# A gated-convolution and attention trunk on one core: the opening of the first layer rebuilt in column quarters

## The reference

```python
mod = silu(c) @ ada_w[l] + ada_b[l]
sh_m, sc_m, g_m, sh_f, sc_f, g_f = split(mod, 6)
h = rms_norm(x, norm_mix_g[l]) * (1 + sc_m) + sh_m
# layer 0: u = h @ sc_w_in[0]; [b_g, c_g, xv] = split(u, 3)
#          y = (b_g * causal_conv3(c_g * xv)) @ sc_w_out[0]
x = x + g_m * y
h = rms_norm(x, norm_mlp_g[l]) * (1 + sc_f) + sh_f
x = x + g_f * (relu(h @ mlp_w1[l]) ** 2 @ mlp_w2[l])
```

## Time and profile before

| | us |
|---|---|
| median of 3 runs (1244.55 to 1245.02) | 1244.95 |
| the profiled execution | 1245.44 |
| its span | 1243.6 |
| PE busy, share of the span | 1188.2, 96% |
| DVE busy, share | 775.5, 62% |
| ACT busy, share | 489.5, 39% |

### The profile page before, as it was taken

One profiled execution on the slowest core, in us unless ns is written; L12 is line 12 of the kernel. 1 busy time (PEld: TensorE's weight loads), 2 busy tenths in 40 slices (PEclk: granted clock), 3 DMA queues, 4 the chain that ended last, 5 costly groups with the idle time before them and its releaser, 6 DMA issues.

```text
span 1243.6 us, 16742 instructions
## 1 busy us (share of the span) xinstructions
PE 1188.2 (96%) x5738; PEld 985.6 (79%) x5738; DVE 775.5 (62%) x1101; ACT 489.5 (39%) x797; POOL 24.7 (2%) x37
## 2 busy tenths in 40 slices
PE   4399999999999999999989999999999999999998
PEld 3288888878888888888868888888888888888887
DVE  5655698886576665555878888787843443443441
ACT  4132242443232232332467777774542232332331
POOL 2000000000000000002020000000000000000000
PEclk9699999999999999999999999999999999999999
DMA  9445666455665656333244455450233333333332
GB/s 338 137 156 200 203 191 192 143 153 190 181 214 176 189 199 202 97 90 87 60 111 120 118 125 131 120 153 18 77 97 98 102 94 92 101 101 86 100 101 85
DMA packets 227294, 168.71 MB, mean 136 GB/s; under 512 B 5316, under 2 KB 206188, under 8 KB 227244
## 3 DMA queue, kind: packets, MB, share of 16 engines
q1 hardware_dynamic: 226684, 165.88, 44.8%
q10 hardware_dynamic: 528, 2.10, 0.5%
q0 software_dynamic: 32, 0.07, 0.0%
HBM read 153.24 MB, written 2.10 MB: 125 GB/s over the span
## 4 chain that ended last, share of the span: by engine, by line
PE 80%; DVE 10%; ACT 4%; issue 3%; DMA 2%; SPq 1%; DVEq 0%; ACTq 0%
PE bank L540 24%; PE bank L542 24%; PE bank L541 24%; PE bank L807 2%; DVE ada_acc L1445 1%; PE bank L789 1%; PE bank L753 1%; DMA raw<-in_sc_w_in 1%; DVE w_lo L1313 1%; DVE h_lo L1362 1%; ACT w_hi L947 1%; DVE ta L1353 1%; PE bank L779 1%; DVE tc L1353 1%; PE bank L780 1%
## 5 line engine op out<-in xcount | busy, mean ns | idle before, releaser
L540 PE MATMUL bank<-h_hi,w_hi 128*128 128x512 f32 (+1 forms) x872 | 340.1, 390 | 23.1 <-DVE h_lo L1362 20.1
L541 PE MATMUL bank<-h_lo,w_hi 128*128 128x512 f32 (+1 forms) x872 | 332.6, 381 | 0.0
L542 PE MATMUL bank<-h_hi,w_lo 128*128 128x512 f32 (+1 forms) x872 | 332.6, 381 | 0.0
L947 ACT ACTIVATE w_hi<-raw 128x1024 fp32r<-128x1024 f32 x188 | 197.4, 1054 | 262.8 <-DMA raw<-in_mlp_w 218.3
L540 PE MATMUL bank<-g_hi,w_hi 128*128 128x512 f32 (+1 forms) x688 | 263.3, 383 | 2.3 <-DVE g_lo L1362 1.5
L1313 DVE TENSOR_TENSOR w_lo<-raw,w_hi 128x1024 fp32r<-128x1024 f32 x188 | 229.4, 1223 | 52.4 <-ACT w_hi L947 47.3
L542 PE MATMUL bank<-g_hi,w_lo 128*128 128x512 f32 (+1 forms) x688 | 257.8, 375 | 0.0
L541 PE MATMUL bank<-g_lo,w_hi 128*128 128x512 f32 (+1 forms) x688 | 257.6, 374 | 0.0
L540 PEld LDWEIGHTS bank<-h_hi,w_hi 128*128 128x128 f32 x872 | 164.9, 189 | 61.1 <-issue 22.9
L541 PEld LDWEIGHTS bank<-h_lo,w_hi 128*128 128x128 f32 x872 | 165.2, 189 | 31.9 <-issue 1.9
L542 PEld LDWEIGHTS bank<-h_hi,w_lo 128*128 128x128 f32 x872 | 164.9, 189 | 31.6
(11 more groups left out here) (172 smaller groups left out, 996.0 us busy)
## 6 DMA issues: line engine op xcount, KB each, us to landing
raw<-in_mlp_w SPq DMA_DIRECT2D x128, 512.0 KB, 4.0
ada_raw<-in_ada_w SPq DMA_DIRECT2D x40, 1024.0 KB, 6.0
raw<-in_sc_w_in SPq DMA_DIRECT2D x24, 512.0 KB, 4.0
ada_first<-in_ada_w SPq DMA_DIRECT2D x16, 512.0 KB, 8.9
raw<-in_w_kv SPq DMA_DIRECT2D x16, 512.0 KB, 4.1
raw<-in_sc_w_out SPq DMA_DIRECT2D x8, 512.0 KB, 4.0
raw<-in_q_w SPq DMA_DIRECT2D x8, 512.0 KB, 4.8
keys<-qk SPq DMA_DIRECT2D x16, 256.0 KB
```

Source lines behind the costliest of these rows:

```text
L540: mm(out[:, cols], weights_hi, hi[:, k, cols], start=(k == 0), stop=False)
L541: mm(out[:, cols], weights_hi, lo[:, k, cols], start=False, stop=False)
L542: return mm(out[:, cols], weights_lo, hi[:, k, cols], start=False, stop=(k == KT - 1))
L947: go(w_hi[:, jj, :, :], raw[:, jj, :, :], ACT.Copy).then_inc(hi_ok, 1)
```

## The change

The first stage is done in four quarters of 256 columns. x comes over SP's queue in four row pieces, ahead of all else; the rows for c, the first norm and the modulation's bias come over ACT's queue; the other rows are loaded and transposed later. ACT squares x by token rows with a running sum, the root is taken on 128 by 4 values, and the token rows are scaled (two by DVE, two by ACT) into x_unit, which PE transposes; ACT turns the transposed tile into h with one scale and shift from PSUM, and copies h_hi. x itself is still transposed and copied, with its own banks. The modulation comes in 32 pieces of 256 KB; DVE takes five pieces of quarter 0 and seven of each other, PE multiplies the remaining ones by silu(c) directly, four products of one column for each piece, and adds DVE's sum with products by ones into the same four columns. Blocks 0 to 3 are open at the same time in banks 0 to 3. Block 4 has buffers of its own (early_raw, early_hi, early_lo) and is split before block 0 is finished. The c_g steps are written out; from step 2 on DVE splits before it does its modulation step. mlp_gain and its like are called after the add of step 3, ahead of that step's weight split.

The diff, cut to its core (its lines moved to the left):

```diff
+QUARTERS = 4
+X_BANK = [0, 1, 2, 3, 7, 7, 7, 7]
+ADA_STEPS = [(0, 1, 2, 3, 4)] + 3 * [tuple(range(KT - 1))]
+ADA_DIRECT = [tuple(k for k in range(KT) if k not in steps) for steps in ADA_STEPS]
+STEP_NO = {(q, k): n for n, (q, k) in enumerate((q, k) for q in range(QUARTERS) for k in ADA_STEPS[q])}
+DIRECT_NO = {(q, k): n for n, (q, k) in enumerate((q, k) for q in range(QUARTERS) for k in ADA_DIRECT[q])}
...
-ada_first, = stacked(region_g, [("ada_first", [P, KT, 2, D // 2], F32)])
+ada_first, = stacked(region_g, [("ada_first", [P, 2, KT, 2, D // QUARTERS], F32)])
...
+c_g = columns(sc_w_in[0], D)
+for t in range(TT):
+    sp.dma_start(x_rows[:, t, :], x_in[0, t * P:(t + 1) * P, :]).then_inc(x_loaded[t], 16)
+def ada_quarter(q):
+    for k in range(KT):
+        if (q - 2, k) in STEP_NO:
+            sp.wait_ge(ada_stepped, STEP_NO[q - 2, k] + 1)
+        elif q >= 2:
+            sp.wait_ge(ada_direct, DIRECT_NO[q - 2, k] + 1)
+        src = ada_w[0, k * P:(k + 1) * P, 0:2 * D].rearrange("p (a q c) -> p a q c", a=2, q=QUARTERS)
+        sp.dma_start(ada_first[:, q % 2, k, :, :], src[:, :, q, :]).then_inc(ada_in[q % 2][k], 16)
+for q in range(QUARTERS):
+    ada_quarter(q)
+    if q < 2:
+        load_block(2 * q, c_g(2 * q))
+        load_block(2 * q + 1, c_g(2 * q + 1))
+sp.wait_ge(hi_ok, 1)
+sp.dma_start(early_raw[:], c_g(GROUP)).then_inc(raw_in[0], 16)
...
-for s in range(2):
-    ada_pair(s, 0, 2, s)
-for s in range(GROUP):
+sp.wait_ge(unit_turned, KT)
+ada_pair(0, 0, 2, 0)
+for s in range(1, GROUP):
     sp.wait_ge(pe_done, s + 1)
     load_block(s, c_g(GROUP + s))
-    if s % 2:
-        sp.wait_ge(ada_used, 2 * KT + s + 1)
-        ada_pair(s // 2, 0, 2, 2 + s // 2)
+    if s == 2:
+        ada_pair(1, 0, 2, 1)
+for s in range(2):
+    sp.wait_ge(ada_used, 2 * KT + 2 * s + 2)
+    ada_pair(s, 0, 2, 2 + s)
 blocks(KT, KT, columns(sc_w_in[0], 2 * D), (0, 3))
...
-pe.wait_ge(rows_in, 16 * 11)
-turn(bank[7][:, 0:ROWS], rows_a[:], ident[0:ROWS, 0:ROWS]).then_inc(cols_pe, 1)
+pe.wait_ge(rows_in, 16 * 3)
+turn(bank[7][:, 0:R_MLP], rows_a[0:R_MLP, :], ident[0:R_MLP, 0:R_MLP]).then_inc(cols_pe, 1)
...
+def unit_pair(q):
+    for i in range(2):
+        j = 2 * q + i
+        if q:
+            pe.wait_ge(hs_ok, j - 1)
+        for t in range(TT):
+            if j == 0:
+                pe.wait_ge(*((unit_ok, t + 1) if t < 2 else (unit_rest_ok, t - 1)))
+            v = turn(bank[4 + i][:, t * P:(t + 1) * P], x_unit[:, t, j * P:(j + 1) * P], ident[:])
+        v.then_inc(unit_turned, 1)
+def quarter_direct(q):
+    if q:
+        pe.wait_ge(ada_red, q)
+    for k in ADA_DIRECT[q]:
+        pe.wait_ge(ada_in[q % 2][k], 16 * (q // 2 + 1))
+        for n in range(4):
+            one = mm(bank[6][:, n:n + 1], ada_first[:, q % 2, k, n // 2, n % 2 * P:(n % 2 + 1) * P],
+                     c_act[:, k:k + 1], start=(k == ADA_DIRECT[q][0] and n == 0), stop=False,
+                     skip_group_check=True)
+        one.then_inc(ada_direct, 1)
+def quarter_sum(q):
+    pe.wait_ge(ada_stepped, STEP_NO[q, ADA_STEPS[q][-1]] + 1)
+    for n in range(4):
+        c = n // 2 * KT + 2 * q + n % 2
+        one = mm(bank[6][:, n:n + 1], ada_acc[:, c * P:(c + 1) * P], ones[:, 0:1], start=False,
+                 stop=True, skip_group_check=True)
+    one.then_inc(ada_turned, 1)
+def x_turn(j):
+    if j == 4:
+        pe.wait_ge(cols_ok, 1)
+    if j > 4:
+        pe.wait_ge(x_ok, j)
     for t in range(TT):
+        if j == 0:
+            pe.wait_ge(x_loaded[t], 16)
+        v = turn(bank[X_BANK[j]][:, t * P:(t + 1) * P], x_rows[:, t, j * P:(j + 1) * P], ident[:])
     v.then_inc(x_turned, 1)
-        add_square(j - 2)
-add_square(KT - 2)
-add_square(KT - 1)
+def open_block(b, tiles):
+    last = part_of(b, b, bank[b], h_hi, h_lo, tiles, lambda k: pe.wait_ge(h_ok, H_MIX0 + k + 1))
+    if tiles[-1] == KT - 1:
+        last.then_inc(pe_done, 1)
 pe.wait_ge(cols_ok, 2)
-ada_turn(0, ADA_HALF)
+pe.wait_ge(c_ok, 1)
+Q = [range(2 * q, 2 * q + 2) for q in range(QUARTERS)]
+for j in range(5):
+    x_turn(j)
+quarter_direct(0)
+unit_pair(0)
+quarter_sum(0)
+x_turn(5)
+pe.wait_ge(x_ok, 4)
+open_block(0, Q[0])
+unit_pair(1)
+quarter_direct(1)
+quarter_sum(1)
+open_block(1, Q[0])
+x_turn(6)
+open_block(0, Q[1])
+open_block(1, Q[1])
+unit_pair(2)
+quarter_direct(2)
+quarter_sum(2)
+open_block(2, Q[0])
+open_block(2, Q[1])
+open_block(3, Q[0])
+x_turn(7)
+open_block(3, Q[1])
+open_block(0, Q[2])
+open_block(1, Q[2])
+unit_pair(3)
+quarter_direct(3)
+quarter_sum(3)
+open_block(2, Q[2])
+open_block(3, Q[2])
+for tile in Q[3]:
+    for b in range(2):
+        open_block(b, range(tile, tile + 1))
+open_block(2, Q[3])
+open_block(3, Q[3])
+pe.wait_ge(rows_more, 16 * 8)
 pe.wait_ge(x_ok, KT)
-ada_turn(ADA_HALF, ADA_GATE)
+turn(bank[7][:, 0:ROWS], rows_a[:], ident[0:ROWS, 0:ROWS]).then_inc(cols_pe, 1)
+dense(1, 0, h_hi, h_lo, weights=(early_hi[:].rearrange("p (s k) c -> p s k c", s=1),
+                                 early_lo[:].rearrange("p (s k) c -> p s k c", s=1)))
+for jj in range(1, GROUP):
+    dense(1, jj, h_hi, h_lo)
...
+def token_square(t):
+    act.wait_ge(x_loaded[t], 16)
+    go(x_unit[:, t, :], x_rows[:, t, :], ACT.Square, accum_out=tok[:, 0, t:t + 1]).then_inc(ms_ok, 1)
+token_square(0)
 act.wait_ge(cols_ok, 1)
 go(c_tmp[:], cols[:, R_C:R_C + KT], ACT.Exp, scale=-1.0).then_inc(silu_e, 1)
+for t in range(1, TT):
+    token_square(t)
+act.wait_ge(consts, C_EPS)
+act.wait_ge(ms_ok, TT)
+link(go(tok[:, 1, :], tok[:, 0, :], ACT.Ln, bias=eps_col[:], scale=1.0 / D))
+go(tok[:, 1, :], tok[:, 1, :], ACT.Exp, scale=-0.5).then_inc(norm_y, 1)
+act.wait_ge(inv_ok, 1)
+for t in range(2, TT):
+    go(x_unit[:, t, :], x_rows[:, t, :], ACT.Copy, scale=tok[:, 3, t:t + 1]).then_inc(unit_rest_ok, 1)
+def first_tile(j):
+    act.wait_ge(unit_turned, j + 1)
+    act.wait_ge(mod_ok, j // 2 + 1)
+    if j >= 4:
+        act.wait_ge(h_ok, H_MIX0 + j - 3)
+    go(hs_slot(j, ALL), bank[4 + j % 2][:], ACT.Identity, bias=mcol(0, 0, j),
+       scale=gains[:, 0, j:j + 1]).then_inc(hs_ok, 1)
+    act.wait_ge(hs_ok, H_MIX0 + j + 1)
+    go(h_hi[:, j, :], hs_slot(j, ALL), ACT.Copy).then_inc(hh_ok, 1)
+def x_tile(j):
     act.wait_ge(x_turned, j + 1)
+    go(x[:, j, :], bank[X_BANK[j]][:], ACT.Copy).then_inc(x_ok, 1)
+def split_early():
+    act.wait_ge(raw_in[0], 32)
+    go(early_hi[:], early_raw[:], ACT.Copy).then_inc(hi_ok, 1)
+split(0, 0)
+for j in range(5):
+    x_tile(j)
+first_tile(0)
+first_tile(1)
+split(0, 1)
+x_tile(5)
+first_tile(2)
+first_tile(3)
+split(0, 2)
+x_tile(6)
+split(0, 3)
+first_tile(4)
+first_tile(5)
+x_tile(7)
+split_early()
+first_tile(6)
+first_tile(7)
...
 def step_cg(g, jj, j):
     act.wait_ge(pe_done, 4 * g + jj + 1)
     go(z[:, bass.ds(j, 1), CONV - 1:] if not isinstance(j, int) else z[:, j:j + 1, CONV - 1:],
        bank[jj][:].rearrange("p (a t) -> p a t", a=1), ACT.Copy).then_inc(bank_free, 1)
-    split(g, jj + 3)
+    if j >= 2:
+        split(g, jj + 3)
...
+def quarter_steps(q, first, last):
+    acc = ada_acc[:, 0:2 * D].rearrange("p (a q c) -> p a q c", a=2, q=QUARTERS)[:, :, q, :]
+    for k in ADA_STEPS[q][first:last]:
+        dve.wait_ge(ada_in[q % 2][k], 16 * (q // 2 + 1))
+        row = ada_first[:, q % 2, k, :, :]
+        if k == 0:
+            one = ts(acc, row, c_act[:, 0:1], None, ALU.mult)
+        else:
+            dve.wait_ge(ada_stepped, STEP_NO[q, k])
+            one = stt(out=acc, in0=row, scalar=c_act[:, k:k + 1], in1=acc, op0=ALU.mult, op1=ALU.add)
+        one.then_inc(ada_stepped, 1)
+def quarter_gain(q):
+    both = lambda t: t[:, 0:2 * KT].rearrange("p (a b) -> p a b", a=2)[:, :, 2 * q:2 * q + 2]
+    dve.wait_ge(ada_turned, q + 1)
+    tt(both(mod), bank[6][:, 0:4].rearrange("p (a b) -> p a b", a=2), both(ada_bias),
+       ALU.add).then_inc(ada_red, 1)
+    dve.wait_ge(ada_red, q + 1)
+    gain(0, 0, 1, R_MIX, q + 1, (2 * q, 2 * q + 2))
+def first_low(j):
+    h_low(H_MIX0 + j, j, None, h_hi, h_lo)
+def split_early():
+    dve.wait_ge(hi_ok, GROUP + 1)
+    tt(early_lo[:], early_raw[:], early_hi[:], ALU.subtract).then_inc(lo_ok, 1)
...
+quarter_steps(0, 0, 2)
+dve.wait_ge(norm_y, 1)
+total, y, half_y2, inv = (tok[:, n, :] for n in range(4))
+link(stt(out=half_y2, in0=y, scalar=-0.5, in1=y, op0=ALU.mult, op1=ALU.mult))
+ts(total, total, 1.0 / D, EPS, ALU.mult, ALU.add).then_inc(norm_v, 1)
+dve.wait_ge(norm_v, 1)
+link(tt(half_y2, half_y2, total, ALU.mult))
+stt(out=inv, in0=half_y2, scalar=1.5, in1=y, op0=ALU.add, op1=ALU.mult).then_inc(inv_ok, 1)
+dve.wait_ge(inv_ok, 1)
+dve.wait_ge(ms_ok, TT)
+for t in range(2):
+    ts(x_unit[:, t, :], x_rows[:, t, :], tok[:, 3, t:t + 1], None, ALU.mult).then_inc(unit_ok, 1)
+quarter_steps(0, 2, 5)
+split(0, 0)
+quarter_gain(0)
+quarter_steps(1, 0, 2)
+first_low(0)
+quarter_steps(1, 2, 3)
+first_low(1)
+split(0, 1)
+quarter_steps(1, 3, KT)
+quarter_steps(2, 0, 2)
+quarter_gain(1)
+quarter_steps(2, 2, 3)
+first_low(2)
+quarter_steps(2, 3, 4)
+first_low(3)
+split(0, 2)
```

(39 more changed lines are left out.)

134 lines of the change are left out of this document (49 added, 85 removed).

## The result

Timed beside the kernel before, the change took 1226.87 us in the median of 4 runs (1225.52 to 1229.58) against 1244.99 (1244.55 to 1245.63): a ratio of 0.9855 with a 95% interval of 0.9842 to 0.9867, so 18.1 us faster. The forecast was 1224.6 with a range of 1219 to 1231. The profiled execution took 1227.90, its span 1226.1.

What follows compares the result with a forecast made beforehand. TensorE, busy 96% of the span, was taken as the bound, with gaps only in the opening. Starting the second group at 61.2 instead of 80.6 saves 19.4, the moved call 0.9: 1244.95 - 20.3 = 1224.6 us, range 1219 to 1231.

Steps and rivals of the forecast that it cites:

- The DMA does not bind here: Opening, quarter 2: its modulation pieces have landed by 34, some 5 us ahead of their last use by DVE.
- Rival (c): Opening's DMA: small runs are slow, 296 GB/s, costing 1.5 to 3 us, so 1226 to 1228; chance 0.07.
- The small rows go over ACT's queue ... no cost: Opening's loads: small rows go ahead of everything on ACT's queue, later stages' rows behind the opening's loads; no cost.
- DVE as the next bound: Opening on DVE: starts at 18.4, a list of work and waits sums to 21.8 us, quarter 2 stepped at 40.2.
- DVE's own end is close beside it: End of first group: h_lo of tile 7 at about 56.5 plus 18 matmuls gives 60.6, beside PE's 61.2.
- PE's list: PE after 40.2: matmuls 16.4, transposes 1.7, thin products 2.4, waits 0.5, so the second group starts at 61.2.
- in the new order PE has work in most of 23 to 40, so I take the full clock from 40.2: PE's clock in the opening: full clock from 40.2 on, with no low-clock loss in the forecast.
- Rival (a): PE from 40.2: low clock for 4 to 5.8 us, losing 2 to 2.9, so 1226.6 to 1227.5; chance 0.14.
- forecast case: Whole kernel: 1224.6 us, own range 1220.5 to 1228; chance 0.66.
- Second group: Blocks after the first four: block 5 ready at 65.1, wanted at 66.7, cover 1.6 us; no cost, narrowly.
- Rival (b): Second group: late weights, block 5 ready at 73.5, PE stands for 6.8 us, about 1231.4; chance 0.06.
- The moved call: mlp_gain ahead of one weight split: PE's 0.86 us wait near 220 goes, saving 0.9; ends nothing or 0.9.

Runs made afterwards that it cites:

- dve_early: The changed kernel with four needless memsets (about 2.5 us of DVE's time) ahead of quarter 2's last steps; one execution, 1231.58 us.
- dve_late: The changed kernel with the same kind of four memsets on DVE ahead of the gain of quarter 3; one execution, 1227.6 us.
- block_first: The changed kernel with block 2's first six matmuls moved ahead of the sum of quarter 2 on PE; 1225.27 us, ratio 0.9842.
- filler: The changed kernel with four unread matmuls of 512 columns on PE ahead of the sum of quarter 2; 1227.15 us, ratio 0.9854.
- no_spare: The changed kernel without block 4's own buffers, block 4 loaded through raw once block 0 is finished; 1235.35 us, ratio 0.9917.
- call_back: The changed kernel with the mlp_gain call put back where it was before; 1230.15 us, ratio 0.9883.

## Why the prediction was right, and where it was off

**The bound and the measure.** "How much earlier the second group starts" held to 0.1 us: 17.56 by the PE timeline, 17.5 by the spans.

**Block 0 and the DMA.** Taken 17.3, measured 17.28. Runs of 1 KB moved at 346 GB/s in the window from 30 to 40, not the 375 taken from between 296 and 388; block 0's landing did not show it, the lag was that much shorter. The rate showed in quarter 2, whose first two pieces DVE waited for, 0.58 and 0.28 us (the DVE timeline above). "The DMA does not bind here" was wrong by 0.9 us, which other terms of DVE's list gave back (its waits for ACT came to 2.1 instead of 2.6). Rival (c) had 296 and 1.5 to 3 us; what it got was under one.

**Norm.** "The small rows go over ACT's queue ... no cost" was wrong in its step and right in its price. The last of them, issued at 1.74, landed at 8.4. Three of ACT's squares stood behind the exponential that needed them; the scalings ended at 15.2 on DVE and 15.9 on ACT instead of 14.2, and quarter 0 was stepped by 17.6 instead of 16.6. Block 0 still landed later, with 0.82 of wait left at DVE: cover of 0.7 had been named, and it was used up by other things than foreseen.

**DVE as the next bound.** Start 18.37 (18.4), quarter 2 stepped by 40.5 (40.2). The sum held to 0.3 us, in part by luck, since a wait for the DMA that it did not have and shorter waits for ACT met in it. dve_early and dve_late, one execution each, bear the reason out: the same 2.5 us delay the sum of quarter 2 and cost nothing behind it. "DVE's own end is close beside it", 0.6 us, was wrong: DVE had 3.90 us to spare at quarter 3's gain, and the h_lo of tile 7 came at 57.87, not 56.5, because it waited for PE.

**PE's list.** From the sum to the second group 21.0 had been worked out (61.2 - 40.2); it took 22.46. The thin products were as taken: eight instructions (each fp32 product shows as two) in 0.95, so 0.24 for a product where 0.2 had been taken. What was missing is the low clock: a wait of 1.05 was followed by 3.4 us with matmuls 0.43 apart, 1.7 lost. block_first and filler took just that away, 1.6 us each behind the sum. The step that failed is "in the new order PE has work in most of 23 to 40, so I take the full clock from 40.2": PE was at full clock at 40.2, but it fell afterwards, at about 42.5, behind a wait that my own list had put there (0.5 of waits was allowed, none of it with a clock behind it). Nor did work bring the full clock as the step supposes: PE was busy without a pause from 22.97, and the clock was low until 35.7. That cost little, since PE still had 1.05 us to wait at the sum.

Rival (a) named the right cost in the right stretch, but it had the clock low on arrival and for 4 to 5.8 us; it was full on arrival, and 3.4 came. The measured 1226.87 lies in rival (a)'s 1226.6 to 1227.5 as well as in the range of the forecast case, so the time alone does not choose between them; the trace does. The sentence of the Trainium skill quoted there (TensorE: Matmul & The Clock Gate, "Part 1: The HAM clock gate"), that activity releases the throttle, fits the standstill before (0.50 from 30 to 40) and the rise at 35.7, but not the fall in this window, in which PE was at work for 1.78 of 2 us and had been without a pause since 10.19:

```profile
18.00:20.00 2.00, 1.78 (x13) 1.69 (x11) 1.39 (x2) 2.00 (x5) 0.00 (x0) 0.66 1.11 342
...
28.00:30.00 2.00, 2.00 (x11) 2.00 (x11) 1.24 (x3) 0.00 (x0) 0.00 (x0) 0.50 1.10 346
```

**Second group.** Block 4 from its own buffers without a wait; block 5 issued from 60.45 on, split by ACT at 64.26 and by DVE from 67.44 to 68.66, wanted at 63.02 + 5.5 = 68.5. PE shows no wait. Rival (b) did not occur: with the queue empty the load landed in under 4 us. The margin was not 1.6 but nearly none. What the spare block is worth had been left unpriced in the forecast; no_spare gives 8.5 us between the medians and 6.7 in its profile.

**The moved call.** Predicted 0.9; by the profiles it is 0 against the kernel before and 0.3 against call_back, whose median is 3.3 higher for a reason not found. I had read one wait (0.86 for mod) and taken it as gained, when behind it, within 15 us, another wait for the same engine stood; DVE's amount of work up to the sum of squares is the same in either order, and PE waits there for what it did not wait for earlier. By the profiles the lower end, "nothing", was the nearer one.

**The sum.** Forecast for the span 20.3, measured 17.5: 0.9 is the call, 1.7 the clock, 0.4 the sum's later start (40.56 for 40.2), and 0.2 came back: the twelve transposes took 1.2 instead of 1.7 and the other waits 0.2 instead of 0.5, the twelve products 2.6 instead of 2.4, and the matmuls the rest.

## What to carry to other kernels

A stall on TensorE can cost more than itself, but not each does. The 1.05 us between thin products cost 2.7 in the profile, the 4.19 of no_spare 6.7. The 1.26 us ahead of 213.99, with dense matmuls of 256 columns up to it, cost only themselves; the clock stayed full around them:

```profile
200.00:230.00 30.00, 27.93 (x207) 26.13 (x206) 24.58 (x50) 12.85 (x26) 0.00 (x0) 1.00 0.48 151
```

When the list shows a wait among thin products ahead of dense work, look for dense work that is ready (here six matmuls of a block already split) and put it in front; that was one moved line and 2.7 us in its profile, though in the median it is not clear of the spread. A wait that one engine imposes on another can only be saved if that engine's work up to the *next* meeting point shrinks; otherwise it turns up there.
